# Block products of two context/latent projections in seven half-size products, and the sums of two norms placed otherwise

## What is computed

```python
def first_block(x, ...):
    ...
    return rms_norm(x, final_g)

def second_block(x, c, ctx, ...):
    xl, xc = x, ctx
    for layer in range(DEPTH):
        hl = modulate(rmsnorm(xl, norm_g[layer, 0]), mod_l[0], mod_l[1])
        hc = modulate(rmsnorm(xc, norm_g[layer, 0]), mod_c[0], mod_c[1])
        # layer 0: even_project, z = h @ w_in for both, and two scans (mLSTM, GLA)
        # layer 1: rwkv_project, r = xr @ w_rkv[0], k = xk @ w_rkv[1], v = xv @ w_rkv[2]
        xl = xl + mod_l[2] * rmsnorm(yl, norm_g[layer, 1])
        hl = modulate(rmsnorm(xl, norm_g[layer, 2]), mod_l[3], mod_l[4])
        xl = xl + mod_l[5] * rmsnorm(conv_ffn(hl, ...), norm_g[layer, 3])
```

## Time and profile before

| | us |
|---|---|
| median of 3 runs (3139.02 to 3143.35) | 3142.51 |
| profiled execution, its own time | 3140.55 |
| its span | 3138.4 |
| PE busy, share of the span | 3000.6, 96% |
| DVE busy | 1225.3, 39% |
| ACT busy | 619.0, 20% |
| POOL busy | 233.1, 7% |
| mean granted TensorE clock | 0.969 |

### The profile page before, as it was taken

How to read it: one execution, slowest core, us unless ns; L and a number is a source line. 1 busy time by engine, 2 the same in 40 slices (tenths; PEclk the granted TensorE clock), 3 DMA queues, 4 the chain that set the end, 5 groups by cost and what they waited for, 6 DMA issues and landing times. The chain is left out here.

```text
span 3138.4 us, 55630 instructions
## 1 busy us (share of the span) xinstructions
PE 3000.6 (96%) x24542; PEld 1936.7 (62%) x24542; DVE 1225.3 (39%) x2528; ACT 619.0 (20%) x1387; POOL 233.1 (7%) x202
## 2 busy tenths in 40 slices
PE   7999999899999999989998999999999799998998
PEld 4889884633333333344576578874554688887887
DVE  3456015311100111025036577761141778874650
ACT  1011013310000000022134221110121555542000
POOL 0000000100000000000012100000000333230000
PEclk8999999899999999989998999999999899998999
DMA  9845548679998899961100342333311100013440
GB/s 385 320 168 211 211 151 333 273 275 384 390 385 347 352 372 387 391 257 67 40 3 1 134 174 81 140 136 126 121 74 37 53 15 27 16 57 149 150 146 14
DMA packets 88499, 577.12 MB, mean 184 GB/s; under 512 B 9536, under 2 KB 15936, under 8 KB 20672
## 3 DMA queue, kind: packets, MB, share of 16 engines
q1 hardware_dynamic: 84800, 568.27, 46.5%
q10 hardware_dynamic: 3456, 5.24, 0.5%
HBM read 567.19 MB, written 6.29 MB: 183 GB/s over the span
## 5 line engine op out<-in xcount | busy, mean ns | idle before, releaser
L273 PE MATMUL ps<-W,ring 128*128 128x256 f32 (+1 forms) x1616 | 490.6, 466 | 8.2 <-DVE W L3472 4.1
L1963 PE MATMUL ps<-ring,W 128*32 128x512 f32 (+1 forms) x2816 | 461.4, 594 | 1.7 <-ACT H L2022 1.7
L273 PE MATMUL ps<-H,ring 128*128 128x256 f32 (+1 forms) x1552 | 429.1, 439 | 7.4 <-ACT H L679 3.7
L273 PEld LDWEIGHTS ps<-W,ring 128*128 128x128 f32 x1616 | 307.9, 191 | 189.9 <-issue 164.7
L273 PEld LDWEIGHTS ps<-H,ring 128*128 128x128 f32 x1552 | 301.1, 195 | 133.9 <-issue 98.0
L1963 PEld LDWEIGHTS ps<-ring,W 128*32 128x32 f32 (+1 forms) x2816 | 142.6, 123 | 306.5 <-issue 303.9
L1986 PE MATMUL ps<-ring,W 128*64 128x512 f32 (+1 forms) x1408 | 231.1, 594 | 0.0
L1986 PEld LDWEIGHTS ps<-ring,W 128*64 128x64 f32 (+1 forms) x1408 | 71.0, 123 | 156.8 <-issue 156.8
L4109 POOL TENSOR_TENSOR ring<-ring 128x512 f32<-128x512 f32 x96 | 132.6, 1401 | 391.9 <-DVE ring L4143 310.5
L2071 DVE TENSOR_TENSOR H<-ps,H 128x256 f32<-128x256 f32 x66 | 28.0, 425 | 303.2 <-ACT H L2013 303.2
L307 PE MATMUL ps<-ring,spread 128*32 128x512 f32 x768 | 104.9, 653 | 20.3 <-DMA ring<-weights 15.9
(11 more groups left out here) (502 smaller groups left out, 3977.8 us busy)
## 6 DMA issues: line engine op xcount, KB each, us to landing
ring<-weights SPq DMA_DIRECT2D x528, 1024.0 KB, 8.1
rkv<-W ACTq DMA_DIRECT2D x16, 256.0 KB, 2.0
ring<-rkv SPq DMA_DIRECT2D x8, 512.0 KB, 3.9
X<-tokens SPq DMA_DIRECT2D x2, 1024.0 KB, 8.6
rkv<-W ACTq DMA_DIRECT2D x8, 128.0 KB, 5.5
W<-rw_tiles SPq DMA_DIRECT2D x4, 256.0 KB, 2.7
ring<-rkv SPq DMA_DIRECT2D x8, 128.0 KB, 4.3
ring<-rw_tiles SPq DMA_DIRECT2D x4, 256.0 KB, 2.6
```

Source lines behind the costliest of these rows:

```text
L273: mm = pe.matmul(out(o), lhsT=k.ring[:, k.slot(at), p * P:(p + 1) * P], rhs=rhs(kk), start=kk == 0 and not (shared_bank and o % 2), stop=k ...
L1963: mm = pe.matmul(ps[at:at + n, r, :], lhsT=moe.Hg[:, kt, FIRST * e + first:FIRST * e + first + n], rhs=w[e][:, kk * WIDE:(kk + 1) * WIDE], ...
```

## The change

1. `Plan` and `Halved` take the first unit, the places of the sums, the banks and the waits as arguments.
2. `stage_even_project`: units 5 to 9 (outputs 10 to 19) are made in seven products each. DVE makes the token sums and the first unit's weight sums behind `decays(1)` and `convolve(8)`. The outputs are combined in place; ACT scales them or puts them through the sigmoid there.
3. `stage_rwkv_project`: units 4 to 11 (keys and values) are made in seven products each; the token sums are made once for the keys and once for the values.
4. `EarlyContext`, `WithContext`: the context's inverse norm is made with that of an earlier stage (out projection and router of the first network), and the normalized and modulated context tiles in the experts' stage, into the space of the `level` constants, which are now loaded at the end of `stage_even_project`. The context halves of outputs 0 to 3 (32 matmuls with 256 tokens) are then placed between the steps of `AfterFirst`; ACT copies the context tiles into `H` behind the latents'.
5. `Weighed` replaces `Ahead` at the end of the RWKV scan: PE sums each squared tile itself, with a 128x2 operand (1 and the squared gate) that gives the sums of both squares at once; POOL and DVE add no squares. The last output is interleaved with these sums.

```diff
-            if kind == 0 and 1 <= u < seven:
+            if kind == 0 and first <= u < seven:
...
+class EarlyContext:
...
+    def vector(self, dve):
+        k = self.k
+        for i in range(KD):
+            dve.tensor_tensor(self.tiles[i], k.X[:, i, CTX], EarlyContext.spread(k), ALU.mult).then_inc(self.normed.sem, 1)
...
+    def copy(self, act):
+        for i in range(KD):
+            act.activation(self.k.H[:, i, CTX], self.tiles[i], ACT.Copy).then_inc(self.copied.sem, 1)
...
+class Weighed(Ahead):
...
+    def square(self, act, o, src):
+        if o >= self.SQUARES:
+            act.wait_ge(self.weighed.sem, self.weighed.at(o - self.SQUARES + 1))
+        act.activation(self.sq[o % self.SQUARES], src, ACT.Square).then_inc(self.squares.sem, 1)
+
+    def add_up_weighed(self, pe, o):
+        if o == 0:
+            pe.wait_ge(self.weights.sem, self.weights.at(1))
+        pe.wait_ge(self.squares.sem, self.squares.at(o + 1))
+        for n, b in enumerate(self.blocks):
+            mm = pe.matmul(self.k.ps[:, self.COLUMNS, 2 * b:2 * b + 2], lhsT=self.sq[o % self.SQUARES][:, n * P:(n + 1) * P],
+                           rhs=self.two[:, o, :], start=self.first_weighed, stop=True, skip_group_check=True)
+            self.first_weighed = False
+        mm.then_inc(self.weighed.sem if o < KD - 1 else self.sums.sem, 1)
...
     def tensor(self, pe, beside):
         k, rms = self.k, self.rms
+        beside(16)
         pe.wait_ge(self.paired.sem, self.paired.at(1))
         rms.add_up(pe, self.pairs[0], rms.blocks)
         pe.wait_ge(rms.squares.sem, rms.squares.at(2 * KD))
         rms.add_up(pe, self.pairs[KD - 1], rms.blocks).then_inc(rms.sums.sem, 1)
+        beside(2)
+        rms.blocks = (2, 3)
         rms.to_all(pe)
+        beside(4)
...
+                if o == 7 and context:
+                    context.tensor(pe, rms)
...
+            def first_free(u):
+                if u < u0 + 2:
+                    pe.wait_ge(sem["conv"], 8)
+                else:
+                    copied(pe, "C11", u - 2)
+
+            def sums_made(u):
+                seven.made(pe, "S2", u)
...
+            gemm(k, pe, 2 * u0 - 4, KD, lambda kk: k.H[:, kk, :], lambda o: ps[:, o % 4, :], before, signals, first=4 * KD)
+            turn_gates()
+            for u in range(u0, un):
+                seven.products(pe, u, B, T3, first_free, sums_made, seventh_free, fifth_free)
...
+            dve.wait_ge(sem["decays"], 4)
+            dve.wait_ge(pre.early.copied.sem, pre.early.copied.at(KD))
+            seven.first_token_sums(dve, B, 0)
+            seven.fourth_token_sum(dve, B, 0)
+            seven.third_token_sum(dve, B, T3)
+            seven.first_sums(dve, u0)
+            seven.second_sum(dve, u0)
+            seven.fourth_sum(dve, u0)
...
-            products([(6, kk) for kk in range(last)])
-            products([(o, last) for o in range(7)] + [(7, kk) for kk in range(KD)])
+            products([(o, last) for o in range(6)])
+            products([(6, kk) for kk in range(KD)])
+            for o in range(6):
+                square.rms.add_up_weighed(pe, o)
+                products([(7, kk) for kk in ((0, 1), (2,), (3,), (4,), (5,), (6, 7))[o]])
+            square.rms.add_up_weighed(pe, 6)
             square.rms.add_totals(pe)
```

More of the change, by code:

```diff
@@ L199, with __init__ @@
 class Plan:
-    def __init__(self, owner, more=0, seven=0, early=0):
+    def __init__(self, owner, more=0, seven=0, early=0, first=1):
         self.product = {}
@@ L776, with __init__ @@
 class AfterFirst(Norm):
-    def __init__(self, k, scale, shift, pairs, g):
-        super().__init__(k, slice(0, T), scale, shift, Rms(k, "after", range(NB), 404, squares=2 * KD))
+    def __init__(self, k, early, scale, shift, pairs, g):
+        super().__init__(k, LAT, scale, shift, Rms(k, "after", range(NB), 404, squares=2 * KD))
+        self.early = early
         self.g, self.pairs = g, pairs
@@ new lines, in take_in_place @@
+            def take_in_place(u):
+                seven.made(act, "C12", u)
+                for o, cols in ((2 * u, LAT), (2 * u + 1, slice(0, T))):
+                    if o not in (11, 12):
+                        take(o, cols, home(o)[:, cols])
+            act.wait_ge(k.mm.sem, k.mm.at(out_done[9]))
+            take(9, slice(0, T), ps[:, 1, :]).then_inc(k.act.sem, 1)
+            act.wait_ge(sem["turned"], 1)
+            for i, (x, f, scale) in enumerate(((ev.c, ACT.Copy, 1.0), (ev.em, ACT.Exp, -1.0))):
+                y = ps[:, 6, 256 * i:256 * i + 256].rearrange("p (b z r) -> p b z r", b=NB, z=2)[:, :, :, 0:4]
+                act.activation(x, y, f, scale=scale).then_inc(sem["turned_out"], 1)
@@ L2801, in _ @@
+            for u in range(u0, un):
+                seven.copy_first(act, u)
+                if u > u0:
+                    take_in_place(u - 1)
+                seven.product_done(act, u, seven.P2)
+                take(2 * u, CTX, seven.first(u)).then_inc(k.act.sem, 1)
+            take_in_place(un - 1)
+            act.wait_ge(k.mm.sem, k.mm.at(out_done[n_out - 1]))
+            take(n_out - 1, slice(0, T), ps[:, 0, :])
             for u in range(m_units):
@@ L3422, in stage_rwkv_project @@
     owner = [i // KD for i in range(27 * KD)]
-    unit_done, out_done, signals, total = plan(owner)
-    last = [7, 15, 23, 24, 25, 26]
+    first, units = 4, 8
+    p = Plan(owner, seven=first + units, first=first)
+    unit_done, out_done, signals, total = p.unit_done, p.out_done, p.signals, p.total
     tokens = lambda n: LAT if n in (0, 5) else slice(0, T)
@@ L3507, in _, with store, receptance @@
-            for o, f in ((24, ACT.Tanh), (25, ACT.Copy)):
-                act.wait_ge(k.mm.sem, k.mm.at(out_done[o]))
-                act.activation(k.X[:, 2 * (o - 24):2 * (o - 24) + 2, CTX],
-                               k.ps[:, o % 4, :].rearrange("p (a t) -> p a t", a=2), f).then_inc(k.act.sem, 1)
+            def store(o):
+                c = tokens(o // 8)
+                act.dma_start(k.a["rkv"][o % 8, :, o // 8, c], out[:, o % 4, c]).then_inc(k.stored[o % 4], 16)
+            def receptance(o):
+                act.wait_ge(k.mm.sem, k.mm.at(out_done[o | 1]))
+                if o >= 4:
+                    free(act, o)
+                act.activation(out[:, o % 4, LAT], place(o), ACT.Copy).then_inc(k.act.sem, 1)
+                copied(act, "r", o)
+                store(o)
@@ new lines, in _ @@
+            for o in range(4):
+                receptance(o)
+            seven.copy_first(act, u0)
+            for o in range(4, 8):
+                receptance(o)
+            for u in range(u0, un):
+                a, b = outputs(u)
+                if u > u0:
+                    seven.copy_first(act, u)
+                    seven.made(act, "C12", u - 1)
+                    copied(act, "C11", u - 1)
+                    store(a - 2)
+                seven.product_done(act, u, seven.P2)
+                free(act, a)
+                act.activation(out[:, a % 4, CTX], seven.first(u), ACT.Copy).then_inc(k.act.sem, 1)
+                seven.made(act, "C21", u)
+                store(b)
@@ L4313, in block1 @@
     moe = Moe(k)
-    stage_router(k, moe, norm1(k, 3, rms), context)
-    return SecondSlots(k, moe, gate(3), stage_experts(k, moe, gate(3)))
+    stage_router(k, moe, norm1(k, 3, rms))
+    early = EarlyContext(k, *parts2(k, 0, 0))
+    return SecondSlots(k, moe, gate(3), stage_experts(k, moe, gate(3), early)), early
 def build(nc, aps):
```

503 lines of the change are left out of this document (357 added, 146 removed).

## The result

| | before | after |
|---|---|---|
| median, us | 3141.48 (4 runs, 3139.02 to 3143.35) | 3123.05 (4 runs, 3120.69 to 3125.91) |
| profiled execution, its own time | 3140.55 | 3120.69 |
| its span | 3138.4 | 3118.9 |

The ratio is 0.9939, 95% interval 0.9923 to 0.9954: faster by 18.4 us in the medians, by 19.5 us in the spans. The forecast was -22.0. The kernel ran again later beside the experiments: 3121.54 us, ratio 0.9939 (0.9925 to 0.9952).

What follows compares the result with a forecast made beforehand. It took PE, busy in 96% of the span, to bound the kernel. Terms of +6.7, -12.0, -11.0, -6.2 and +0.5 summed to -22.0 us, giving a median of 3120.5 us, range 3109 to 3132.

Steps and rivals of the forecast that it cites:

- Seven products, 13 units: Even projection (5 units) and RWKV (8): 12.09 us a unit instead of 13.76, gaining 8.3 and 13.3 us.
- the rule that the prediction weighed: Trainium skill: weight loads overlap matmuls only on other array rows; by it each seven-product unit would lose 3 us net.
- First unit of the even projection: Unit 5: PE waits 7.7 and 5.3 us for DVE's late sums, clock loses 2.0; stage from output 4 on +6.7 us.
- RWKV: RWKV projection: eight units gain 13.3 us, the first waits 1.3 us; sum -12.0 us (-13.3 to -9).
- The norm between the networks: Early context matmuls fill PE's wait for DVE's pair sums and keep PE warm: -11 us (-13.4 to -8.4).
- the clock case that I had held for a bound: Norm: low clock in the first 3.5 us, in the sums and behind them costs 5 us (1.7 + 1.7 + 1.7).
- End of the scan: RWKV scan's end: POOL's and DVE's 6.4 us queue goes, fewer records in the next stage; -6.2 us (-8 to -2).
- Small: Context's two sum matmuls move from under a wait in the router to a dense stretch: 4 records, +0.5 us.
- No lag: Rival, even projection: DVE gets to S2 in time or the wait is filled; -37 us, 3105 us; chance 0.06.
- The clock case: Rival: low clock eats the closed waits at norm, unit 5 and scan's end; -11.4 us, 3131 us; chance 0.17.
- Every unit waiting: Rival, all 13 units: DVE late for C22; at 3.3 us late each, +21 us, 3163 us; chance 0.03.
- weight loads in the open: Rival: 24 more loads a unit not hidden, 4.6 us each unit; +38 us, 3180 us; chance 0.01.

Runs made afterwards that it cites:

- Without the block: Changed kernel with PE's test of the count of second slots and the code it skips left out, on PE alone: 3115.74 us, ratio 0.9921.

## Why the prediction was right, and where it wasn't

- **Seven products, 13 units: right.** 12.08 to 12.09 us a unit in both stages; 12.09 was forecast. One unit more or less moved the stretch by 1.65 us. The weight loads cost nothing, against the rule that the prediction weighed. One reading was off: the 3.8 us of the earlier trace rows are idle time of the weight loads' queue (PEld); PE itself had none ahead of L2299, which speaks for the same term even more strongly.
- **First unit of the even projection: right in its event, off in one detail.** S2 was forecast 14.7 us behind the transposes and came after 14.44. The second wait was 2.87 us and not 5.3, because the first product ran at 1.2 GHz and took 3.75; the sum is the same, since S2 alone sets it. Clock behind it: 16 records in 6.09 us instead of 3.62, 2.5 us against the 2.0 taken. +6.92 for +6.7. (The prediction put the rise of the clock in the earlier trace rows some 3.5 us into dense matmuls; from the rows it is 3.2, from 1400.88 to about 1404.1. The sum doesn't hang on it.)
- **RWKV: right.** One wait of 1.17 us for 1.3; C22 waited 1.67 us for the store, and behind it PE has no bracket. -11.70 for -12.0.
- **The norm between the networks: the mechanism right, the size wrong.** It gave -7.43, outside the bounds of -13.4 to -8.4. The step that failed is "ACT begins at 1386.15, PE's queue can too": I took ACT's 1386.15 - 1384.42 = 1.7 us for PE too. In the trace of before PE's start there was hidden beneath the 7.71 us for DVE, so no row of the timeline showed it; the section on time and profile before was too sure that another engine had always just ended what PE waited for. It was 5.69 us, 4.0 more, and with it the first third of the clock case that I had held for a bound came true (1.8 us). Without the block the stretch shortens by 45.70 - 31.59 = 14.1 us, the -13.4 of the undisturbed sum and 0.9 us for an even earlier start, to 0.2 us: the rest of the term was sized rightly. By the prediction's own mark this part fell, since less than 8 us were gained, and two of its signs didn't come: L2794 within 2 us of the stage's begin, and outputs 0 to 3 ending some 30 us behind it. The total held because 3.6 us are little among 22, and because shared stretches gave 1.6 us back, which was luck. This part of the change was not taken back as a whole in any run; its -7.43 is read from the stretch.
- **End of the scan: right.** -6.14 for -6.2; no bracket above 0.75 us ahead of L734 or L675, and none for POOL.
- **Small: right.** The stage with the context's sums is 19.24 us long instead of 18.79.
- The remaining -2.45 - 0.45 + 0.33 + 1.01 = -1.6 us isn't put down to the change. In twelve profiles of the changed kernel and its variants the same row (L2063) began between 1369.42 and 1372.56 us, and the scan, equal in all of them up to its end, took 425.8 to 428.9; the values of before, 1372.13 and 427.87, lie in these ranges. With one profile of before, a small real part can't be excluded, such as the load of constants that went from the start.
- **The rivals.** "No lag" was the likeliest way to be much faster, and didn't come; with one unit later it does. The clock case was to leave the norm -8.4, the even projection +9, RWKV -10.5 and the scan's end -2; measured were -7.43, +6.92, -11.70 and -6.14, so it held for the norm alone, and there the late start did more than the clock. Every unit waiting and weight loads in the open are out by the pitch of 12.08 us.

## What to carry to other kernels

When a cheaper form replaces work, look first at what the old work covered: outputs 10 and 11 were the cover of DVE's lag, and starting the cheap form one unit later gives up 1.7 us for 15.2; that version, 3109.7 us, beats both kernels, as does two units later, 3106.8. Two brackets in a row may be one lag: find the event behind the last of them and ask when that comes. And before an engine's work is moved to the start of a stage, ask when that engine can start, from a row of its own. Behind a long wait the timeline of before can't show it, and another engine's start is no measure; whether code is skipped there, and whether a packet of instructions falls into the wait, can be looked up.

## What the runs showed of the hardware

- PE got over a skipped block at a cost of a step: 2.04 us with an empty body, 2.30 with 56 products in it, 5.35 with 126 (one profile each), 5.3 to 6.9 with 180 (eight profiles). A packet of 16 KB of PE's code falls into each of the long idle times, two into the two longest, none into the short ones. ACT and DVE, whose blocks to skip are shorter, stood idle 1.73 us (behind PE's last product) and 1.82 us (behind DVE's own).
- Behind 2.04 us of idle time the granted clock fell to 0.50 (1.2 GHz) within PE's first products, behind 0.84 us it stayed at 1.00.
- Stages that two kernels share exactly differ from execution to execution by up to 3.1 us (the scan: 425.76 and 428.88 us in two profiles of one program). Three stretches that came back when a part of the change was taken back agreed with before to 0.1 us (122.97 and 122.97, 157.43 and 157.53, 30.83 and 30.83). Where a term is a few us, the stretch tells it and the whole time doesn't.
